# Column vectors to broadcast rows: turned by TensorE and written in contiguous rows, in place of element-by-element writes

## The reference, cut to what matters

```python
mod = einsum('bd,de->be', silu(c), w_ada) + b_ada
shift1, scale1, gate1, shift2, scale2, gate2 = split(mod, 6)
h  = norm(x) * (1 + scale1) + shift1 ...
x  = x + gate2[:, None, :] * y2        # first network: gate2 times PEER's output
x  = x + gate * (rms(y) * g_post)      # second network, after attention and after the feed-forward part
```

## Time and profile before

| | us |
|---|---|
| median of 3 runs (lowest, highest) | 2424.52 (2424.47, 2427.72) |
| the profiled execution, its own time | 2428.97 |
| its span, first to last instruction | 2426.9 |
| TensorE matmuls busy | 2186.9 |
| TensorE weight loads busy | 1956.3 |
| VectorE busy | 1720.8 |
| ScalarE busy | 1145.6 |
| GpSimd busy | 62.8 |
| mean granted TensorE clock | 0.954 of full speed |

### The profile page before, as it was taken

One profiled execution on the slowest core, in us unless ns is written; L12 is line 12 of the kernel. 1 busy time (PEld: TensorE's weight loads), 2 busy tenths in 40 slices (PEclk: granted clock), 3 DMA queues, 4 the chain that ended last, 5 costly groups with the idle time before them and its releaser, 6 DMA issues.

```text
span 2426.9 us, 37729 instructions
## 1 busy us (share of the span) xinstructions
PE 2186.9 (90%) x14566; PEld 1956.3 (81%) x14566; DVE 1720.8 (71%) x3370; ACT 1145.6 (47%) x1941; POOL 62.8 (3%) x79
## 2 busy tenths in 40 slices
PE   3998889999999999989986979799989988797998
PEld 2987889999987778878865656799989978567997
DVE  5667669889988877787865666587776665665554
ACT  2643344555554445454444445444454445354444
POOL 1000000000000000000010000000000000000000
PEclk9999989999999999999988989899999999898999
DMA  7647645664458877777841110477767753104664
GB/s 281 198 133 266 196 150 192 211 219 133 146 185 271 263 257 260 264 246 233 261 109 47 58 57 18 139 246 248 243 215 256 250 173 126 53 1 122 186 187 131
DMA packets 139216, 438.70 MB, mean 181 GB/s; under 512 B 15712, under 2 KB 38496, under 8 KB 138528
## 3 DMA queue, kind: packets, MB, share of 16 engines
q1 hardware_dynamic: 109440, 396.93, 51.3%
q10 hardware_dynamic: 25776, 23.97, 2.9%
q0 software_dynamic: 3824, 15.40, 1.9%
HBM read 422.58 MB, written 13.66 MB: 180 GB/s over the span
## 4 chain that ended last, share of the span: by engine, by line
PE 48%; DVE 15%; issue 11%; DMA 9%; ACT 5%; POOL 0%; ACTq 0%; DVEq 0%; POOLq 0%; SPq 0%
PE bk L1765 45%; DVE SPL L1140 4%; DMA TMP<-kept 3%; DMA RAW<-in_peer 3%; PE bk L1771 3%; ACT SPL L789 2%; ACT R L791 1%; DVE RAW L1174 1%; DMA kept<-TMP 1%; DVE ST L1155 1%; DVE TMP L1140 1%; DVE R L1149 1%; ACT R L789 1%; DMA HID<-kept 1%; DVE EXT L1174 1%
## 5 line engine op out<-in xcount | busy, mean ns | idle before, releaser
L1140 DVE TENSOR_TENSOR SPL<-RAW,SPL 128x1024 fp32r<-128x1024 f32 (+1 forms) x614 | 744.1, 1218 | 361.4 <-ACT SPL L789 359.5
L789 ACT ACTIVATE SPL<-RAW 128x1024 fp32r<-128x1024 f32 (+1 forms) x614 | 644.8, 1054 | 620.1 <-PE bk L1765 297.0
L1765 PE MATMUL bk<-HH,SPL 128*128 128x256 f32 x3840 | 748.8, 289 | 28.8 <-DVE HL L1140 13.8
L1765 PEld LDWEIGHTS bk<-HH,SPL 128*128 128x128 f32 x3840 | 622.3, 194 | 36.1 <-DVE HL L1140 14.3
L1765 PE MATMUL bk<-SPL,WHL 128*128 128x512 f32 x2328 | 553.9, 391 | 12.5 <-DVE WHL L1140 6.8
L1765 PE MATMUL bk<-HL,SPL 128*128 128x256 f32 x1920 | 548.1, 285 | 0.0
L1765 PEld LDWEIGHTS bk<-SPL,WHL 128*128 128x128 f32 x2328 | 428.3, 188 | 106.0 <-issue 19.2
L1765 PEld LDWEIGHTS bk<-HL,SPL 128*128 128x128 f32 x1920 | 373.4, 194 | 2.4
L1765 PE MATMUL bk<-SPL,HH 128*128 128x256 f32 (+1 forms) x1664 | 316.4, 292 | 32.3 <-DVE SPL L1140 20.1
L1765 PEld LDWEIGHTS bk<-SPL,HH 128*128 128x128 f32 x1664 | 270.0, 200 | 40.7 <-issue 27.2
L789 ACT ACTIVATE R<-bk 128x256 f32<-128x256 f32 (+4 forms) x350 | 170.4, 498 | 232.9 <-PE bk L1765 186.1
(11 more groups left out here) (132 smaller groups left out, 1939.4 us busy)
## 6 DMA issues: line engine op xcount, KB each, us to landing
RAW<-in_peer SPq DMA_DIRECT2D x256, 512.0 KB, 4.8
RAW<-in_ada SPq DMA_DIRECT2D x144, 512.0 KB, 4.8
RAW<-in_ffn SPq DMA_DIRECT2D x132, 512.0 KB, 4.3
RAW<-in_win SPq DMA_DIRECT2D x96, 512.0 KB, 4.6
RAW<-in_ffd SPq DMA_DIRECT2D x66, 512.0 KB, 4.4
RAW<-in_wout SPq DMA_DIRECT2D x32, 512.0 KB, 4.6
kept<-TMP ACTq DMA_DIRECT2D x88, 128.0 KB, 3.2
TMP<-kept ACTq DMA_DIRECT2D x66, 128.0 KB, 5.6
```

Source lines behind the costliest of these rows:

```text
L789: ins = e.activation(out, in_, func, bias=bias, scale=scale)
L1140: e.tensor_tensor(out, a, b, op).then_inc(*dve.up(*points))
L1765: ins = e.matmul(out, lhsT, rhs, start=start, stop=stop, skip_group_check=True)
```

## The change

A new step `vt` (l) stands behind `mods` (l, "f") in the plan. TensorE turns two pieces of `MOD` and `AB` (104 and 64 columns for layer 0, 48 and 32 for layer 1), ACT copies them out of the bank to `TMP`, and POOL writes them to `vec` as rows of 128 contiguous numbers in two transfers. All seven `keep_row` writes go, `A2` and `mods` on POOL with them. PEER's gate is among layer 0's columns, so its write moves from step `A2` to `vt` 0. Its read (`row_of("peer", gB2)`) moves from `c_in` to the end of POOL's `vt` 0. Each read takes 8 consecutive rows of `vec` and waits for both writes of its layer.

```diff
-    peer += late + [("mods", 0, "f")]
+    peer += late + [("mods", 0, "f"), ("vt", 0)]
...
-    ffn = weave(ffn_steps(0, 0)[:-3], last[24:]) + [("mods", 1, "f")]
+    ffn = weave(ffn_steps(0, 0)[:-3], last[24:]) + [("mods", 1, "f"), ("vt", 1)]
...
+        turned_mod = {0: MOD[:, 40:144], 1: MOD[:, 144:192]}
+        turned_ab = {0: AB[:, 32:96], 1: AB[:, 96:128]}
...
-            def keep_row(key, src):
-                e.dma_start(vec_d[VECS[key]].rearrange("(k p) -> p k", p=P), src,
-                            allow_slow_non_contiguous=True).then_inc(...)
+            def turn_rows(l):                                   # POOL
+                pool.wait_ge(T.at("out", ("vt", l)))
+                n, m = turned_mod[l].shape[1], turned_ab[l].shape[1]
+                e.dma_start(vec_d[l, 0:n, :], TMP[0:n, 2560:2688]).then_inc(*T.up(f"d_mod{l}", 16, [("vm", l)]))
+                e.dma_start(vec_d[l, 104:104 + m, :], TMP[0:m, 2688:2816]).then_inc(*T.up(f"d_ab{l}", 16, [("vec", l)]))
+                if l == 0:
+                    row_of("peer", gB2)
             def row_of(key, dst):
-                pool.wait_ge(T.at("vec", key))
-                e.dma_start(dst, vec_d[VECS[key]].partition_broadcast(P)).then_inc(...)
+                l, a = VECS[key]
+                pool.wait_ge(T.at("vm", l), T.at("vec", l))
+                e.dma_start(dst, vec_d[l, a:a + 8, :].rearrange("k p -> (k p)").partition_broadcast(P)).then_inc(...)
-            def a2():
-                pool.wait_ge(T.at("A2"))
-                keep_row("peer", MOD[:, 40:48])
-            def mods_(l, part):
-                ...
             def c_in():
                 pool.wait_ge(T.at("mul", ("peer", 99)), T.at("saved"))
-                row_of("peer", gB2)
                 load("x3", R[:, 0:2048], xs_d[:, :])
...
+            def turn_rows(l):                                   # ACT
+                key, n, m = ("vt", l), turned_mod[l].shape[1], turned_ab[l].shape[1]
+                act.wait_ge(T.at("full", key))
+                A(TMP[0:n, 2560:2688], ps(*key)[0:n, 0:P], ACT.Copy)
+                A(TMP[0:m, 2688:2816], ps(*key)[0:m, P:2 * P], ACT.Copy, ("out", key))
...
+            def turn_rows(l):                                   # TensorE
+                b = take(("vt", l), (6, 7))
+                pe.wait_ge(T.at("mods", l, "f"))
+                e.transpose(b[0:turned_mod[l].shape[1], 0:P], turned_mod[l], ident)
+                e.transpose(b[0:turned_ab[l].shape[1], P:2 * P], turned_ab[l], ident).then_inc(*pe.up(("full", ("vt", l))))
```

More of the change, by code:

```diff
@@ L418, in modulation @@
                                   for s in ((1, 0) if both else (0,))]
-        VECS = {"peer": 0, (0, 0, "a"): 1, (0, 0, "f"): 2, (0, 1, "a"): 3, (0, 1, "f"): 4, (1, 0, "a"): 5, (1, 0, "f"): 6}
+        turned_mod = {0: MOD[:, 40:144], 1: MOD[:, 144:192]}
+        turned_ab = {0: AB[:, 32:96], 1: AB[:, 96:128]}
+        VECS = {"peer": (0, 0)}
+        for l in range(2):
+            for s in range(2):
+                VECS[(l, s, "a")], VECS[(l, s, "f")] = (l, 112 + 32 * s), (l, 128 + 32 * s)
+                VECS[(l, s, "f", "A")], VECS[(l, s, "f", "B")] = (l, 120 + 32 * s), (l, 48 * s + 24 + (0 if l else 8))
         first_ctx = PLAN.index(("norm_b", (0, 1, "a")))
@@ L718, in top_in @@
                 e.dma_start(xs_d[:, :], X).then_inc(*T.up("d_xs", 16, [("saved",)]))
-            def keep_row(key, src):
-                e.dma_start(vec_d[VECS[key]].rearrange("(k p) -> p k", p=P), src,
-                            allow_slow_non_contiguous=True).then_inc(*T.up(f"d_vec{VECS[key]}", 16, [("vec", key)]))
-            def row_of(key, dst):
-                pool.wait_ge(T.at("vec", key))
-                e.dma_start(dst, vec_d[VECS[key]].partition_broadcast(P)).then_inc(*T.up(f"d_row{VECS[key]}", 16, [("row", key)]))
-            def a2():
-                pool.wait_ge(T.at("A2"))
-                keep_row("peer", MOD[:, 40:48])
-            def mods_(l, part):
[L734 to L738, removed]
+            def turn_rows(l):
[5 more added lines that the diff above has]
+                    row_of("peer", gB2)
+            def row_of(key, dst):
+                l, a = VECS[key]
+                pool.wait_ge(T.at("vm", l), T.at("vec", l))
+                name = "d_row" + "_".join(str(k) for k in key)
+                e.dma_start(dst, vec_d[l, a:a + 8, :].rearrange("k p -> (k p)").partition_broadcast(P)).then_inc(
+                    *T.up(name, 16, [("row", key)]))
             def gB(l, s, k):
@@ L773, in df_a @@
                 power(stat(144, 8, s), stat(136, 8, s), 8, "diff", l, s)
-            steps = {"A2": a2, "mods": mods_, "gB": gB, "sil": sil, "sil2": sil2, "norm_a": norm, "norm_k": norm, "mix_in": mix_in, "AT": at_, "ln": ln, "on": on,
+            steps = {"vt": turn_rows, "gB": gB, "sil": sil, "sil2": sil2, "norm_a": norm, "norm_k": norm, "mix_in": mix_in, "AT": at_, "ln": ln, "on": on,
                      "top_in": top_in, "c_in": c_in, "nT": nT, "scl": scl, "gn_a": gn_a,
@@ L1116, in scalar_program @@
                      "ktT": ktT_, "AT": at_, "ln": ln, "o": o_, "gB1": gB1_, "mT": mT, "wq": wq, "sc": sc, "pick": pick,
-                     "selT": selT, "g": g, "pe": pe_, "pl": pl, "ph": ph, "fz": fz, "pd": pd, "lam": lam, "pj": pj, "scl": scl, "lr1": lr1,
+                     "selT": selT, "g": g, "pe": pe_, "pl": pl, "ph": ph, "fz": fz, "pd": pd, "vt": turn_rows, "lam": lam, "pj": pj, "scl": scl, "lr1": lr1,
                      "lr2": lr2, "tr": tr_, "as": as_, "at": at, "ao": ao, "ad": ad, "dT": dT, "op": op, "wout": wout,
@@ L2070, in tensor_program @@
                      "o": o_, "sgu": sgu, "gB1": gB1_, "mT": mT, "wout": wout, "wq": wq, "sc": sc, "selT": selT, "g": g,
-                     "pe": pe_, "pd": pd, "pu": pu, "pj": pj, "lr1": lr1, "lr2": lr2, "tr": tr_, "as": as_, "at": at,
+                     "pe": pe_, "pd": pd, "pu": pu, "vt": turn_rows, "pj": pj, "lr1": lr1, "lr2": lr2, "tr": tr_, "as": as_, "at": at,
                      "av": av, "dq": dq, "dT": dT, "op": op, "fh": fh, "fy": fy}
@@ L2166, in make @@
         kept = nc.dram_tensor("kept", (NA, P, 256), F32, kind="Internal").ap()
-        vec = nc.dram_tensor("vec", (7, D), F32, kind="Internal").ap()
+        vec = nc.dram_tensor("vec", (2, 168, P), F32, kind="Internal").ap()
         program(nc, dram, out, xs, kept, vec, points)
```

## The result

| | before | after |
|---|---|---|
| median of the runs, us | 2424.49 (2421.24 to 2427.97, 6 runs) | 2440.47 (2436.15 to 2443.2, 6 runs) |
| profiled execution, us | 2428.97 | 2441.78 |
| its span, us | 2426.9 | 2439.7 |
| its mean granted clock | 0.954 | 0.955 |

The ratio is 1.0059, 95% interval 1.0042 to 1.0075: the changed kernel is slower by 14.3 us (10.2 to 18.2). The ratios given here are estimates with intervals; the quotient of two medians differs from them a little (here 1.0066). The forecast was +10.6 us, 2435.1, in a range from 2430.5 to 2441.5. A second measurement, `r2_after_again`, gave 1.0050 (1.0035 to 1.0065), 12.1 us.

The account below looks back on a forecast made before the run. The prediction found no single engine the limit, and DVE without a gap around 1220 us. Its terms 9.7 + 1.3 - 0.4 = +10.6 us, added to the median 2424.5, gave 2435.1 us, range 2430.5 to 2441.5.

Parts of the forecast that it names:

- What bounds it: Near 1220 us the chain is on DVE without a gap, with no slack between `mods` and `peer_out`.
- The new wait, +9.7 us: Near 1220 us PEER's row travels between `mods` and `peer_out`, which starts 9.7 us late, all passed on; bounds 8.9 and 13.2.
- The price of a small write: Landing of POOL's second row write near 1222 us: 3.2 us taken, bounds 2.7 and 4.0, far end 9.7.
- The rival of slow small writes: Second write near 1222 us lands after 9.7 us whatever its form; sum +17.1 us, 2441.6; chance 0.10.
- TensorE's clock, 0: Behind the gap near 1229 us the low clock comes in either case; value 0, bounds 0 and 2 us.
- `c_in`, -0.4 us: Near 1016 us the 512 KB read leaves POOL's queue; the weight load gains 0.4 us, bounds 0 and -1.3.
- The rival of a large relief: At `c_in` the removed read held up the weight load; chain 7.2 us shorter, net +3.8, 2428.3; chance 0.08.
- Layer 1, +1.3 us: Near 1976 us two transposes and two ACT copies delay the squares of `fo`: +1.3 us, bounds 0.6 and 1.5.
- The bank rotation, "value 0": One more user between `vt` 0 and `vt` 1 exchanges banks 6 and 7 later; a microsecond either way, value 0.
- The writes that go: Element-by-element writes, at 272 and 1220 us among others, are slow but nobody waits for one; removing them gains nothing.

Follow-up runs that it names:

- r2_after_again: The changed kernel again, unchanged, for a second trace: 2435.18 us, ratio 1.0050 to the kernel before.
- e2_read_late: The kernel before with only the read of PEER's row moved behind `mods` (0, "f"), ahead of the four element-by-element writes: 2434.46 us, ratio 1.0047.
- e5_two_reads: The changed kernel, but POOL reads PEER's row twice in sequence and DVE waits for the second read: 2443.95 us, ratio 1.0081.
- e8_read_alone: The kernel before with PEER's row read behind `mods` (0, "f") and the four element-by-element writes put off by some 97 us: 2428.9 us, ratio 1.0021.
- e6_own_rotation: The changed kernel with a bank rotation counter of its own for `vt`, so later steps keep their former banks: 2433.97 us, ratio 1.0043.
- e4_all_early: The changed kernel with PEER's gate turned and written early, its row read at 1087 us, `vt` 1 behind the norm after `fo`: 2426.61 us, ratio 1.0019.
- e9_early_all_own_bank: `e4_all_early` with a bank rotation counter of its own for `vt`: 2425.32 us, ratio 1.0001 to the kernel before.
- e3_pe_filled: The changed kernel with 40 unused transposes of the identity on TensorE ahead of `as` 0, into bank 5: 2437.63 us, ratio 1.0052.
- e10_exchange_only: The kernel before with only the counter of bank rotation (6, 7) put one further at the places of `vt` 0 and `vt` 1: 2425.8 us, ratio 1.0017.
- e7: `e1` with a bank rotation counter of its own for `vt`: 2424.67 us, ratio 1.0006 to the kernel before.
- e1: The changed kernel, but PEER's gate is written element by element at `A2` and read in `c_in` as before: 2428.45 us, ratio 1.0022.

## Why the prediction was right, and where not

- **What bounds it.** No slack between `mods` and `peer_out`, as the earlier trace rows said: shown by `e2_read_late`, `e5_two_reads` and `e8_read_alone`, which change hardly more than that wait and pass it on. Nothing of it is given back soon: from `peer_out`'s start to 1294.6 of before seven traces with a wait take 73.4 to 76.2 us, seven without 72.8 to 75.6.
- **The new wait, +9.7 us.** 9.74 in the trace, 10.61 in the second. Step by step from the end of `mods`, forecast and measured: bank full 0.5 and 0.6 us, the second write issued 2.1 and 1.9, its landing 3.2 and 3.3, the read's 4.2 and 4.0, and 0.5 of POOL's wake-up where 0.2 stood. `e6_own_rotation`, the change without the exchange, loses 10.4 us (6.5 to 14.3), where the other terms add up to 10.6 as forecast and to 9.7 as measured.
- **The price of a small write.** Taken from 128 KB out of ACT's queue, 3.2 us; 52 and 32 KB from POOL's took 3.7 and 3.3. The rival of slow small writes falls. PEER's gate alone shows it best, with the same 4 KB in both forms: 8 rows of 512 bytes land in 5.0 and 4.3 us (`e4_all_early`, `e9_early_all_own_bank`), 1024 elements in 8.3 to 10.6 (the traces that write it at `A2`). By the prediction's estimate from the Trainium skill, "DMA: Bandwidth & Descriptors", Anatomy of one DMA, the write would take 2.1 us and the read 3.2; the trace has 3.3 and 4.0, and the rows were the better guide.
- **TensorE's clock, 0.** Right in size: it is low for some 14 us (1228.3 to 1242.0) instead of 7 (1229.1 to 1235.9), but through work that DVE bounds for most of it. The projection began at 1238.54 and met the low level for 3.5 us, where before it began at 1230.45 and met it for 5.5. `e3_pe_filled`, meant as the test, left the size open.
- **`c_in`, -0.4 us.** From 1010 to 1090 us five traces with the read there take 79.9 us in the mean, nine without it 79.5 (77.7 to 80.3). The sign and size agree, within a spread that could hide them. (Four other loads stand behind the read in `c_in`, not five.) The rival of a large relief falls: 11.29 us are left of 12.01, and ACT's waits for such loads, below, are 8.8 us where the earlier trace rows had 7.6.
- **Layer 1, +1.3 us: mis-sized.** It measured some +0.4: from `fo` to a fixed DVE instruction at 2000 us, 23.1 to 23.2 us in five traces without `vt` 1 ahead of `fo` and 23.4 to 23.6 in the seven with it (in `e4` and `e9`, where it stands behind the norm, 23.8 and 24.4). Two transposes take 0.23 us in the chain, not 0.4, and two ACT copies 0.42, not 0.8. A plain copy takes 0.27 us and the next starts 0.17 behind its start; the passes of the earlier trace rows, which also take a scale and a shift from `AB` and `MOD`, take 0.45 each, 0.34 apart, and were the wrong row to go by. The squares, which begin 0.68 us behind the last product and not 1.3, took 2.27 us where before they took 2.43.
- **The bank rotation, "value 0": the step that failed.** Its bounds were a microsecond either way, and it costs 4.1 us (1.0 to 7.3) by `e10_exchange_only`, of which 1.4 are shown as a wait, with `e7` and `e9` against `e1` and `e4` pointing the same way, 0.16 and 0.18%. I saw that two banks change places and didn't ask who stands in each, when it is copied out, and behind what on ACT.
- **The writes that go.** Right that they bring nothing: `e7_early_own_bank` is at 1.0006, `e9_early_all_own_bank` at 1.0001. The rule on contiguous rows that the prediction cites (the Trainium skill, "DMA: Bandwidth & Descriptors", Rules for kernel authors) holds for the transfer (8.3 to 13.7 us in the traces with element-by-element writes, 2.6 to 5.2 with rows) and says nothing of the kernel's time.

```profile
ACT SPL L790 <- DMA RAW<-in_peer: 8.8, 3, 4.6
```

With the measured sizes the sum is 9.7 + 4.1 + 0.4 - 0.4 = 13.8 us, against 14.3 and 12.1 in the two measurements; the intervals of these and of the 4.1 are wide enough that the closeness is partly chance. The forecast was right in its main mechanism, the wait. It was 3.7 us short of the first measurement and 1.5 of the second, since it left out one term of 4.1 and had another 0.9 too large. That the median, 2440.47, lies in the range owes something to luck: it is 1 us below the upper end, which had been set for a slower round trip and slow writes, and the exchange of banks brought it there.

## What to carry to other kernels

A slow transfer that nobody waited for cost nothing here. Before making one faster, look at who waits for it and when. If the faster form needs an engine's later product, count the whole round trip at its new place (here 9.7 us, of which 7.3 were two landings). One `take` more in a shared rotation changes the banks of every later step: give a new user a counter of its own, or read who holds each bank at that time and which in-order engine empties it. Where both can be avoided, compare the cleaned form with the kernel before; here it came out equal, so the old form could stay.

## What was unexpected of the hardware

- Element-by-element writes hold up a read that was issued ahead of them on the same queue: 9.5 us for 512 KB with four of them issued behind it from 0.5 us on, 5.9 without, with ring loads running beside both. Nearly all of the difference lies between the read's last packet and its landing, 3.4 us against 0.3.
- In this kernel a bank rotation with one count more and no other change costs 0.17% of the time (0.04 to 0.30).
- The clock stayed at 1.00 while TensorE was busy 0.22 of 2 us (1224 to 1226) and 1.20 of 2 (1226 to 1228) in `e3_pe_filled`, and was at 0.50 from 1230 on. Forty transposes that ended 11 us ahead of the projection gained it nothing.
- Between 1342 and 1500 us traces of equal work differ by 4 us according to where a stretch of low clock begins and how long such stretches last (27.3 to 40.6 us in all). What sets the place was not found.
